# The last head and the output projection of a latent-attention layer: products between the steps, outputs split in place, norm by root

## What is computed

```python
o = mla_attend(q[..., :QK_NOPE], rope(q[..., QK_NOPE:], pos))      # per head: softmax(scores) @ v
x = x + (o * jax.nn.silu(p[..., Q_LORA:])) @ b_w_out               # gate, output projection 1024 x 1024, residual
y = x * rsqrt(mean(x * x) + EPS) * final_norm                      # the final norm
```

## Time and profile before

| | |
|---|---|
| median of three runs | 1352.81 us |
| the profiled execution: time / span | 1353.24 us / 1351.5 us |
| TensorE busy | 1285.9 us, 95% |
| VectorE / ScalarE / GpSimd busy | 708.9 / 438.9 / 529.5 us |
| mean granted clock | 0.985 |
| last head's last scores to the last store | about 1217 to 1351.5 us |

### The profile page before, as it was taken

One profiled execution on the slowest core, in us unless ns is written; L12 is line 12 of the kernel. 1 busy time (PEld: TensorE's weight loads), 2 busy tenths in 40 slices (PEclk: granted clock), 3 DMA queues, 4 the chain that ended last, 5 costly groups with the idle time before them and its releaser, 6 DMA issues. The chain is left out here.

```text
span 1351.5 us, 21509 instructions
## 1 busy us (share of the span) xinstructions
PE 1285.9 (95%) x8573; PEld 1244.9 (92%) x8573; DVE 708.9 (52%) x1369; ACT 438.9 (32%) x845; POOL 529.5 (39%) x590
## 2 busy tenths in 40 slices
PE   6999999999999999989999999899999999997995
PEld 6999999999999999979999999789999999997994
DVE  7367463446335543574333587365666556666134
ACT  6324232223223232352123322243444344432122
POOL 2344433425262516154566555402222131236423
PEclk9999999999999999999999999899999999998998
DMA  5231222212122111035232158602301322135112
GB/s 212 95 101 51 76 65 85 72 56 76 55 92 75 57 63 59 21 147 191 98 113 80 35 177 277 190 13 65 73 31 47 73 65 49 29 127 195 52 50 81
DMA packets 54227, 120.65 MB, mean 89 GB/s; under 512 B 12416, under 2 KB 29056, under 8 KB 53872
## 3 DMA queue, kind: packets, MB, share of 16 engines
q1 hardware_dynamic: 51552, 110.11, 24.7%
q0 software_dynamic: 2576, 9.18, 2.5%
HBM read 80.57 MB, written 35.89 MB: 86 GB/s over the span
## 5 line engine op out<-in xcount | busy, mean ns | idle before, releaser
L83 PE MATMUL psum<-act,fox_slot_hi 128*128 128x358 f32 (+1 forms) x552 | 183.0, 331 | 10.3 <-DVE act L976 10.3
L84 PE MATMUL psum<-act,fox_slot_hi 128*128 128x358 f32 (+1 forms) x552 | 180.2, 326 | 0.0
L85 PE MATMUL psum<-act,fox_slot_lo 128*128 128x358 f32 (+1 forms) x552 | 180.0, 326 | 0.0
L1302 POOL TENSOR_SCALAR fox_rows<-fox_f_keys,fox_f_query 128x144 f32<-128x144 f32 (+3 forms) x64 | 50.3, 787 | 177.1 <-PE psum L691 174.5
L83 PEld LDWEIGHTS psum<-act,fox_slot_hi 128*128 128x128 f32 x552 | 104.2, 189 | 10.4 <-DVE act L976 10.3
L84 PEld LDWEIGHTS psum<-act,fox_slot_hi 128*128 128x128 f32 x552 | 104.2, 189 | 0.0
L85 PEld LDWEIGHTS psum<-act,fox_slot_lo 128*128 128x128 f32 x552 | 104.1, 189 | 0.0
L871 ACT ACTIVATE fox_pT_hi<-psum 128x512 fp32r<-128x512 f32 (+3 forms) x112 | 52.4, 504 | 103.8 <-PE psum L691 103.8
L849 ACT ACTIVATE fox_rows<-fox_rows,fox_neg_max 128x144 f32<-128x144 f32 (+3 forms) x64 | 50.6, 791 | 97.1 <-DVE fox_neg_max L1057 96.2
L83 PE MATMUL psum<-fox_slot_hi,act 128*128 128x256 f32 (+1 forms) x288 | 81.1, 282 | 0.0
L85 PE MATMUL psum<-fox_slot_hi,act 128*128 128x256 f32 (+1 forms) x288 | 81.0, 281 | 0.0
(11 more groups left out here) (410 smaller groups left out, 3977.0 us busy)
## 6 DMA issues: line engine op xcount, KB each, us to landing
fox_x<-in_xT SPq DMA_DIRECT2D x8, 536.0 KB, 9.7
out<-fox_key SPq DMA_DIRECT2D x8, 536.0 KB, 2.7
mix_resid<-in_xT SPq DMA_DIRECT2D x8, 536.0 KB, 3.9
resid_b<-mix_resid SPq DMA_DIRECT2D x8, 536.0 KB, 2.9
q_nope<-mla_nope SPq DMA_DIRECT2D x8, 536.0 KB, 5.1
mla_query<-q_nope SPq DMA_DIRECT2D x8, 536.0 KB, 5.7
fox_f_keys<-f_cum SPq DMA_DIRECT2D x8, 520.0 KB, 4.1
fox_stage<-in_fox_wk SPq DMA_DIRECT2D x8, 512.0 KB, 3.5
```

The costliest lines, as they stand in the source:

```text
L83: pe.matmul(out, lh, rh, start=start and k == 0, stop=False)
L84: pe.matmul(out, lh, rl, start=False, stop=False)
L85: last = pe.matmul(out, ll, rh, start=False, stop=stop and k == n - 1)
L1302: chain(pool.tensor_scalar(row[:, KEY_META:KEY_META + live], f_keys[h % 2][:, 0:live], 1.0, f_query[:, i + 1, h:h + 1], ALU.mult, ALU.add))
```

## The change

All of it concerns the last head (h = 7) and the output projection.

- The three gate chunks of the last head move from steps 1, 2, 3 to steps 0, 1, 2.
- Heads 0 to 6: ScalarE rounds each output (hi) within steps 3 to 6, GpSimd subtracts and writes the rest (lo) in place of the output. The residual rows move to the place of attention's first buffers, so SyncE loads them after the last output is ready.
- The eighth head is split by column chunk: ScalarE and VectorE split the first two chunks before the last `values` has ended.
- Blocks 0 and 1 of chunk 0: the pieces of heads 0 to 6 are multiplied between the steps (heads 0 and 1 in step 6 ahead of its transposes, 2 and 3 and then 4 and 5 in step 7, 6 ahead of the last `values`), into the two banks of the projections.
- GpSimd waits for the last gate multiply before it splits weight block 2. The loads of weight blocks 2 and 4 (the third and the fifth) are issued earlier.
- The norm: Sqrt on ScalarE and a reciprocal on VectorE in place of Ln and Exp; the mean is taken after block 1, the factor after block 3 of the next chunk, and finishing is spread over blocks 4 to 7.
- In the last chunk GpSimd finishes two blocks instead of three, multiplies their gains before the factor is there, and ScalarE issues their stores.

```diff
-    return [] if h == 0 else ({1: [0], 2: [1], 3: [2]} if h + 1 == HEADS else {1: [0], 3: [1], 5: [2]}).get(i, [])
+    return [] if h == 0 else ({0: [0], 1: [1], 2: [2]} if h + 1 == HEADS else {1: [0], 3: [1], 5: [2]}).get(i, [])
...
+        o_hi = [r.take(f"end_o_hi{k}", [P, T], F32R, ACT_BASE + 28 * T + 4 * T * k) for k in range(HEADS)]
+        o_lo = [r.take(f"end_o_lo{k}", [P, T], F32R, ACT_BASE + 4 * T * k) for k in range(HEADS - 1)] + [at(59104, f"end_o_lo{HEADS - 1}", [P, T], F32R)]
         o_raw = [r.take(f"end_o{k}", [P, T], F32, ACT_BASE + 4 * T * k) for k in range(HEADS - 1)] + [query_32]
-        y = o_raw[0:KT - 1] + [gate]
+        y = [at(4 * T * fb, f"end_y{fb}", [P, T]) for fb in range(KT)]
...
-        LATE = 5
+        LATE = 6
+        END_BANKS = (6, 7, 0, 1, 2, 5)
...
+        def end_product(pe, c, fb, ks):
+            use = end_use(c, fb)
+            col, w = END_CHUNKS[c]
+            for k in ks:
+                if k == HEADS - 1:
+                    pe.wait_ge(own_o_split, c + 1)
+                elif use < 2:
+                    pe.wait_ge(o_split, k + 1)
+                if k == 0:
+                    pe.wait_ge(end_split, fb + 1)
...
+        def round_o(act, k):
+            act.wait_ge(o_loaded[k], 16)
+            act.activation(o_hi[k][:, :], o_raw[k][:, :], ACT.Copy).then_inc(o_rounded, 1)
...
+                act.activation(end_sum[c % 2][:, 0:w], end_mean[:, 0:w], ACT.Sqrt).then_inc(end_root, 1)
+
+            round_own_o(act, 2)
             for c in range(3):
                 for fb in range(KT):
                     square_y(c, fb)
-                    if c and fb == 3:
-                        roots(c - 1)
-            roots(2)
+                    if c and fb == 1:
+                        root(c - 1)
+            root(2)
+            for fb in range(LATE, KT):
+                col, w = END_CHUNKS[2]
+                act.wait_ge(y_done_late, KT - LATE + fb - LATE + 1)
+                act.dma_start(dram.y_out[fb * P:fb * P + P, col:col + w], y[fb][:, col:col + w]).then_inc(y_stored_late, 16)
...
-                dve.wait_ge(end_root, 2 * c + 2)
+                dve.wait_ge(end_root, c + 1)
+                dve.reciprocal(f, t).then_inc(end_step, 1)
...
+            def rest_o(k):
+                pool.wait_ge(o_rounded, k + 1)
+                pool.tensor_tensor(o_lo[k][:, :], o_raw[k][:, :], o_hi[k][:, :].bitcast(F32), ALU.subtract).then_inc(o_split, 1)
...
-            for k in range(4):
-                split_o(k)
+            pool.memset(o_raw[HEADS - 1][:, N_SAMPLE:SMALL], 0.0).then_inc(o_cleared, 1)
+            pool.wait_ge(gate_ready, 3 * HEADS)
             split_w(2)
+            for k in range(HEADS - 1):
+                rest_o(k)
             pool.wait_ge(out_full, last_out)
             pool.memset(end_ones[:, :], 1.0).then_inc(end_ready, 1)
             split_w(3)
...
+            load_w(2)
             sp.wait_ge(proj_full[proj.bank(last_gate)], proj.nth(last_gate) + 1)
...
             for k in range(HEADS - 1):
                 sp.dma_start(o_raw[k][:, :], dram.gated_b[k * DH:k * DH + DH, :]).then_inc(o_loaded[k], 16)
-            load_w(2)
             load_w(3)
-            sp.wait_ge(o_first_split, 4)
+            load_w(4)
+            sp.wait_ge(out_ready, last_out)
             for fb in range(4):
                 load_y(fb)
-            load_w(4)
-            sp.wait_ge(out_ready, last_out)
-            load_y(KT - 1)
-            sp.wait_ge(o_split, 8)
-            for fb in range(4, KT - 1):
+            load_w(5)
+            for fb in range(4, KT):
                 load_y(fb)
-            for n in range(5, KT):
+            for n in range(6, KT):
                 load_w(n)
...
+                    if h + 1 == HEADS:
+                        for k in {6: (0, 1), 7: (2, 3)}.get(i, ()):
+                            for fb in range(2):
+                                end_product(pe, 0, fb, [k])
                     if i % 2:
                         turn_probs(h, i, TURNS_FIRST)
...
+                    if h + 1 == HEADS and i == 7:
+                        for k in (4, 5):
+                            for fb in range(2):
+                                end_product(pe, 0, fb, [k])
...
+            for fb in range(2):
+                end_product(pe, 0, fb, [6])
             values(HEADS - 1, 3)
             end_pe(pe)
...
+                    if h + 1 == HEADS:
+                        for k in {3: (0,), 4: (1, 2), 5: (3, 4), 6: (5, 6)}.get(i, ()):
+                            round_o(act, k)
+            round_own_o(act, 1)
             end_act(act)
```

More of the change, by code:

```diff
@@ L1664, in square_y, with root @@
                 act.activation(dst[:, 0:w], y[fb][:, col:col + w], ACT.Square).then_inc(y_squared, 1)
-            def roots(c):
+            def root(c):
                 w = END_CHUNKS[c][1]
                 act.wait_ge(end_meaned, c + 1)
-                act.activation(end_sum[c % 2][:, 0:w], end_mean[:, 0:w], ACT.Ln).then_inc(end_root, 1)
-                act.wait_ge(end_root, 2 * c + 1)
-                act.activation(end_rms[c % 2][:, 0:w], end_sum[c % 2][:, 0:w], ACT.Exp, scale=-0.5).then_inc(end_root, 1)
-            act.wait_ge(out_full, last_out)
-            for cols in (slice(0, EW), slice(EW, T)):
-                for k in range(4, HEADS):
-                    round_o(k, cols)
+                act.activation(end_sum[c % 2][:, 0:w], end_mean[:, 0:w], ACT.Sqrt).then_inc(end_root, 1)
+            round_own_o(act, 2)
             for c in range(3):
@@ L1714, in finish @@
                                          op1=ALU.mult).then_inc(y_done, 1)
-            for n, cols in enumerate((slice(0, EW), slice(EW, T))):
-                for k in range(4, HEADS):
-                    dve.wait_ge(o_rounded, 4 * n + k - 3)
-                    dve.tensor_tensor(o_lo[k][:, cols], o_raw[k][:, cols], o_hi[k][:, cols].bitcast(F32), ALU.subtract).then_inc(o_split, 1)
+            rest_own_o(dve, 2)
+            done = {4: (0, 1), 5: (2, 3, 4), 6: (5, 6), 7: (7,)}
             for c in range(3):
@@ L1722, in end_dve @@
                     add(c, fb)
-                    if c and fb == 2:
+                    if c and fb == 1:
                         mean(c - 1)
-                    if c and fb == 4:
+                    if c and fb == 3:
                         factor(c - 1)
-                    if c and fb >= 4:
-                        finish(c - 1, 2 * fb - 8)
-                        finish(c - 1, 2 * fb - 7)
+                    for q in done.get(fb, ()) if c else ():
+                        finish(c - 1, q)
             mean(2)
@@ L2577, in _ @@
                         split_query(h + 1)
+                    if h + 1 == HEADS and i == 7:
+                        round_own_o(act, 0)
                     if i % 2:
@@ L2755, in _ @@
                         gate_sample(h)
+            rest_own_o(dve, 0)
+            rest_own_o(dve, 1)
             gated(HEADS - 1, 3)
```

88 lines of the change are left out of this document (40 added, 48 removed).

## The result

The changed kernel takes 1339.8 us (median of four runs, 1338.9 to 1343.6) against 1352.3 before (four runs; the 1352.8 ahead of the prediction was of three); the ratio is 0.9907, 95% interval 0.9891 to 0.9924. That is 12.5 us or 0.9% less; 1342.3 was predicted, with 1337.0 to 1348.5 as the range.

The account below looks back on a forecast made before the run. Bound: TensorE's idle and low clock ahead of its full last stretch, 11.5 us. 11.5 - 0.8 - 1.75 - 0.4 - 1.6 + 0.3 + 0.0 + 3.2 = 10.45 us less, so 1342.3; range 1337.0 to 1348.5.

Parts of the forecast that it names:

- The pieces fill the idle, and the clock stays: Last head's steps 6 and 7 to chunk 0: moved products remove TensorE's idle and low clock, 11.5 us at most.
- late low halves: Steps 6 and 7: products cannot start where put, TensorE waits in step 7 as now; 1347.9 us, chance 0.07.
- a fallen clock: Steps 4 to 7: rescales fully held, scattered idle brings TensorE's clock to 0.56; 1362.4 us, chance 0.05.
- the signs: From step 6 to block 7: one TensorE run with idles under 1 us and clock 1.00 would show the forecast right.
- Gate a step earlier: Step 3 of the last head: new TensorE idle ahead of scores(7,5), 0.8 us lost (0 to 1.3).
- Locks: Steps 4 to 7: GpSimd's subtractions hold VectorE's rescales and TensorE waits, 1.75 us lost (0 to 4).
- Seventh head's low part: Last head: GpSimd's subtraction for the seventh head ends after TensorE wants it, 0.4 us lost (0 to 1.1).
- Weight chain: Output projection, blocks 5 to 7: weight blocks come late behind residual loads and sums, 1.6 us lost (0 to 4).
- Earlier chunks' finish: Last chunk: VectorE does mean, factor and finish of earlier chunks one block earlier, 0.3 us gained (0 to 0.4).
- Root: Last mean to factor: root and reciprocal replace Ln, table load and Exp; 0.0 us gained (-1.2 to 1.2).
- Stores: Kernel's end: gains multiplied beforehand, two blocks on GpSimd, last store issued sooner; 3.2 us gained (2.6 at six of 0.7).
- rival 1: Last head to end: filling is whole, engines rarely meet, weights in time, reciprocal cheap; 1337.4 us, chance 0.20.

Follow-up runs that it names:

- the copies: GpSimd's seven subtractions of the outputs replaced by one-operand copies in place, against the changed kernel; median 1339.4 us, 152.3 us for the stretch against 153.5.
- the second profile: The changed kernel run and profiled once more with nothing altered; median 1340.8 us, 153.8 us for the stretch against 153.5.

## Why the prediction was right, point by point

- **The pieces fill the idle, and the clock stays.** Right. 11.5 us were put down as loss; undoing this part alone brings back 6.4 us of idle and the clock of 0.56. The rivals of late low halves and of a fallen clock did not come. Of the signs, the clock is 1.00 throughout, but one idle is over 1 us (1.23).
- **Gate a step earlier: 0.8.** Right in place and kind, 0.56 measured. What it buys was left unpriced, and is over 2 us: without it ScalarE stands 2.67 us at the first load. That GpSimd's wait for the gate multiply guards the clock too (0.51 without it) was priced nowhere.
- **Locks: 1.75 forecast, about 0.5 measured.** This term was mis-sized. The rescales are held as worked out (1.3, 1.4 and 2.0 forecast; 1.4, 1.75 and 1.9 by the difference to the freed ones, 0.56, 0.69 and 0.76). TensorE's waits for that are 0.18 at step 5 (0.6 forecast), 0.31 ahead of scores(7,7), less than the 0.45 of the earlier trace rows (0.65 forecast), and 0.43 in step 7 (0.95). Why the waits are so much shorter than worked out stays open: with two of the rescales freed by the copies, only the 0.43 goes.
- **Seventh head's low part: 0.4.** 0.58 measured.
- **Weight chain: 1.6, at blocks 5 to 7.** 1.23 measured (1.51 in the second profile), all at block 6. Block 5 was in time there, though it waits 0.41 to 0.81 us in three of the edited kernels; block 6 waited for its transfer, and with that one ahead nothing waits. The order of the transfers, not the amount of GpSimd's work, is the limit. The prediction had both, the transfers as the reason for blocks 6 and 7.
- **Sum of these:** costs of 2.8 instead of 4.55 on 11.5 us; 8.1 measured for the first part against 6.95 forecast, or 7.25 with the gain of 0.3 below. Windows from the anchor to the last mean, before and after:

```profile
1185.62:1336.01 150.39, 141.98 (x863) 137.38 (x863) 67.26 (x111) 38.80 (x72) 63.22 (x46) 0.97 0.28 104
```

```profile
1188.33:1330.59 142.26, 138.46 (x863) 133.56 (x863) 64.83 (x107) 36.57 (x68) 66.65 (x47) 1.00 0.30 111
```

  TensorE's idle falls by 4.6 us (8.41 to 3.80), and the same 863 matmuls take 3.5 us less at the higher clock. The idle comes out as forecast (5.28 and 2.1 less costs of 2.8); the clock had been put down at 4.1 (2.4 and 1.7), and that is the 0.6 between 11.5 - 2.8 = 8.7 and 8.1.
- **Earlier chunks' finish: 0.3.** Block 7's sum waits for TensorE now and is no longer late, as forecast. From the start of the last product to that of the mean there are 1.98 us instead of 2.13 (1328.61 to 1330.59, 1333.88 to 1336.01): 0.15 measured.
- **Root: 0.0.** 4.07 before and after, and 4.08 with Ln and Exp in the new place. The reciprocal taken at 1.6 is 1.75, and one table load is left of six, as forecast; that 1.6, a middle between two far rows, came out so near is luck. By the Trainium skill (ScalarE: Activation LUTs, Table sets: the hidden batching unit) a pair of Ln and Exp needs one load. The trace disagrees in the kernel with Ln and Exp too: two loads of 1.28 us for each of three pairs, and the second stands on the chain. The 2.1 us estimated from the repeat count of 8 in the Trainium skill (VectorE: DVE Perf Modes, First, the fixed hardware budget) is over what was measured: 1.75 for 256 columns and 2.69 for 408, some 6 ns for each further column.
- **Stores: 3.2 forecast, 4.3 measured.** The six blocks take 3.40 us, as forecast. Mis-sized is what lies behind the last issue: taken over as 4.8 us from GpSimd's, it is 3.5 with SyncE's (the last store's row starts at 1338.26). SyncE's stores land in 1.7 to 1.9 us, GpSimd's in 2.0 to 2.4, which is 0.2 to 0.3 of the difference of 1.2. The rest is GpSimd itself. The instructions with which the engines of the kernel before leave its block (L1491; count, ns min/median/max, first and last start):

```profile
L1491 POOLq EVENT_SEMAPHORE  x4: 17/17/17, 1350.0 to 1351.4; - x4
L1491 POOLq DRAIN  x3: 40/250/3227, 1346.7 to 1351.2; - x3
L1491 SPq DRAIN  x2: 7/7/7, 1349.0 to 1350.2; - x2
```

  Beside its last issue GpSimd stands in a drain of 3.23 us from 1346.70 to 1349.93, and only then do the engines' closing semaphores begin, 0.96 us after SyncE was through with its waits for the stores (1349.01). In the changed kernel the two starts are 1340.30 and 1340.27; with the end undone the drain of 3.23 us and the 0.96 are back.
- **The scale.** 10.45 forecast, 12.4 in the stretch, 12.5 between the medians. The two mis-sized terms (1.25 of locks, 1.1 behind the last issue) make 2.35; the others (gate 0.2 and weight chain 0.4 less, low part 0.2 more, finish 0.15 and clock 0.6 short) take some 0.3 of it back, which leaves the 2.0 of difference. The time lies 0.3 us inside the lower edge of the forecast (1339.5 to 1345.0), about midway between the sum and rival 1, though none of rival 1's conditions held: GpSimd and VectorE met, a weight block came late, and the reciprocal was not cheap. That it fell on this side of the edge is luck.

## What to carry to other kernels

Work that depends on little is best kept for the place where a dependent chain leaves the matrix engine idle: it wins the idle, what the clock loses behind it (3.5 of 8.1 us here), and it covers waits that the same edit creates on other engines. An edit that starts something earlier should be followed to the transfers it depends on: here the longest wait that was left came from a transfer queued behind 2.1 MB of residual rows, which could come 2 us later without a cost to TensorE. The engine that issues a kernel's last store matters too: GpSimd's drain held the end up by 1 us. And to judge parts of one us in a kernel of 1340 us that scatters by 5, measure from an anchor inside the trace to the end, not the whole.

## What was not expected of the hardware

- That GpSimd's instructions hold VectorE's rescales was forecast from the earlier trace rows; how far it reaches was not. A subtraction of two operands (2.4 to 2.8 us) holds a VectorE instruction that neither reads nor writes `psum`, by up to 2.0 us: the rescale of 1044 columns takes 2.71 beside it and 0.76 without, the gate multiply 2.26 instead of 0.52, the subtraction of 408 columns 2.79 instead of 0.54. A GpSimd instruction with one operand holds it too (1.18 instead of 0.63). VectorE's instructions that read the matrix engine's results (L2674, L2697, L2708) are not longer in the same stretch.
- At the end the two engines share: 6 + 2 blocks take VectorE 3.40 us, 5 + 3 take 3.47.
- A store issued by GpSimd at the very end costs a drain of 3.23 us on GpSimd, for which the closing semaphores wait, 0.96 us longer than for the stores.
- An idle of 2.30 us on TensorE was followed by a clock of 0.51, idles of 2.60 and 3.19 were followed by 1.00.
- The reciprocal costs some 6 ns for each further column on VectorE (1.75 us at 256, 2.69 at 408), where the mean and the steps of correction take 0.42 and 0.58.
